# Where eight and eight page loads are issued: behind the compression's last product and at the head of the prompt's stage

## The reference, cut to what matters

```
comp = compress_blocks(...)                       # blocks of 64 rows through a two-layer net with a gelu
o_c, p_c = cmp_attend(q, pos_q, comp, slopes)     # scores on the compressed blocks
idx = select_blocks(sum(p_c), pos_q, nb)          # the 16 best blocks
o_s = slc_attend(q, pos_q, gather_sel(idx), ...)  # attention inside the chosen blocks
o_w = win_attend(q, pos_q, kv_win, pos_win, ...)  # the last 512 tokens
o = gate0 * o_c + gate1 * o_s + gate2 * o_w
```

## Time and profile before

| | |
|---|---|
| median of 3 runs | 907.37 us (906.33 to 907.95) |
| the profiled execution | 907.63 us, of it 905.8 us span |
| TensorE busy | 839.6 us, 93% of the span |
| DVE, ACT, POOL busy | 417.6, 335.0, 129.4 us |
| bytes moved | 102.96 MB, 33.56 MB of them on POOL's queue |
| mean granted TensorE clock | 0.967 of full speed |

### The profile page before, as it was taken

The page is one execution under the profiler, slowest core; times in us unless marked ns, Lnnn a source line. Parts: engine busy times, 40 slices in busy tenths (PEclk is TensorE's granted clock), DMA queues, the critical chain, the costliest instruction groups (busy, mean ns, idle before and its releaser), DMA issues.

```text
span 905.8 us, 17118 instructions
## 1 busy us (share of the span) xinstructions
PE 839.6 (93%) x7279; PEld 760.4 (84%) x7279; DVE 417.6 (46%) x776; ACT 335.0 (37%) x618; POOL 129.4 (14%) x157
## 2 busy tenths in 40 slices
PE   5999998997888878897999999999999999999995
PEld 4999977774555645566999999999999999999995
DVE  5435646665555475565327433344333433243432
ACT  6501155553566564454225431043212331043311
POOL 0001101100784325520220000000000000000120
PEclk9999999997999888998999999999999999999998
DMA  8922638832570206517221122222221122222002
GB/s 299 322 72 94 192 84 272 269 119 93 163 205 8 82 1 233 193 61 189 94 94 41 55 91 93 93 93 93 93 84 37 64 93 93 93 94 93 1 1 105
DMA packets 48789, 102.96 MB, mean 114 GB/s; under 512 B 7498, under 2 KB 19166, under 8 KB 46429
## 3 DMA queue, kind: packets, MB, share of 16 engines
q1 hardware_dynamic: 41821, 68.61, 22.9%
q0 software_dynamic: 6912, 33.56, 11.0%
HBM read 97.75 MB, written 8.53 MB: 117 GB/s over the span
## 4 chain that ended last, share of the span: by engine, by line
PE 52%; DVE 1%; ACT 0%; DVEq 0%; issue 0%
PE banks L1981 51%; PE banks L2022 0%; DVE y L1971 0%; PE banks L2048 0%; DVE wl L1901 0%; PE banks L2038 0%; ACT wh L1845 0%; DVE hT L1939 0%; DVE hT L1914 0%; DVE xl L1918 0%; ACT low L1859 0%; DVE xl L1907 0%; ACT xh L1861 0%; DVEq L1794 0%; ACT small L1889 0%
## 5 line engine op out<-in xcount | busy, mean ns | idle before, releaser
L1981 PE MATMUL banks<-xh,wh 128*128 128x288 f32 x640 | 138.0, 297 | 4.3 <-DVE xl L1907 3.9
L1981 PE MATMUL banks<-xl,wh 128*128 128x288 f32 x640 | 137.8, 297 | 0.0
L1981 PE MATMUL banks<-xh,wl 128*128 128x288 f32 x640 | 137.7, 297 | 0.0
L1845 ACT ACTIVATE wh<-low 128x1024 fp32r<-128x1024 f32 x72 | 75.0, 1050 | 103.1 <-PE banks L1981 102.8
L1981 PE MATMUL banks<-ah,wh 128*128 128x288 f32 x512 | 110.1, 297 | 0.0
L1981 PE MATMUL banks<-ah,wl 128*128 128x288 f32 x512 | 109.7, 296 | 0.0
L1981 PE MATMUL banks<-al,wh 128*128 128x288 f32 x512 | 109.6, 296 | 0.0
L1981 PEld LDWEIGHTS banks<-xh,wh 128*128 128x128 f32 x640 | 103.8, 190 | 4.9 <-DVE wl L1901 4.1
L1981 PEld LDWEIGHTS banks<-xh,wl 128*128 128x128 f32 x640 | 103.9, 190 | 0.0
L1981 PEld LDWEIGHTS banks<-xl,wh 128*128 128x128 f32 x640 | 103.9, 190 | 0.0
L1939 DVE TENSOR_TENSOR hT<-banks,hT 128x288 f32<-128x288 f32 x64 | 26.3, 453 | 138.9 <-PE banks L1981 138.9
(11 more groups left out here) (330 smaller groups left out, 1383.2 us busy)
## 6 DMA issues: line engine op xcount, KB each, us to landing
low<-in_w_up SPq DMA_DIRECT2D x8, 2048.0 KB, 7.8
low<-in_w_down SPq DMA_DIRECT2D x8, 2048.0 KB, 7.7
zone<-in_cmp_w SPq DMA_DIRECT2D x16, 256.0 KB
o_swin<-in_state_win SPq DMA_DIRECT2D x8, 504.0 KB
px<-in_x_prompt SPq DMA_DIRECT2D x4, 512.0 KB, 5.3
u_raw<-in_w_in SPq DMA_DIRECT2D x1, 2048.0 KB, 10.0
q_raw<-in_w_in SPq DMA_DIRECT2D x1, 2048.0 KB, 10.3
low<-in_state_win SPq DMA_DIRECT2D x4, 512.0 KB
```

The source lines that it names most:

```text
L1845: act.activation(wcols(m.wh, i), raw_cols(i), ACT.Copy).then_inc(wh_ready, 1)
L1981: last = pe.matmul(out(i, hf), w[wi], half(x[:, k, :], hf), start=first and part == 0, stop=end and part == 2)
```

## The change

Eight loads of pair 0 go to the end of POOL's part of the compression, behind a new wait on the last product. Eight loads of pair 1 go to the head of POOL's part of the prompt's stage, behind the memset. The loop keeps none. The loads themselves, their places and their semaphores are the same, 16 in all.

```diff
@@ on_gpsimd of compress @@
             load_chunk(pool, m, sems, ck)
+        pool.wait_ge(hid_done, UNITS)
+        for x in range(4):
+            for e in range(2):
+                load_pages(pool, m, 0, e, x, sems)
@@ POOL's part of prompt @@
             pool.memset(m.kc2, 0.0).then_inc(sems.cleared, 1)
-            loads = [(n, e, x) for n in range(2) for x in range(4) for e in range(2)]
+            for x in range(4):
+                for e in range(2):
+                    load_pages(pool, m, 1, e, x, sems)
             for t in range(HPG * U):
                 pool.wait_ge(scl_ready, t + 1)
...
                 last.then_inc(scaled, 1)
-                if 1 <= t <= len(loads):
-                    n, e, x = loads[t - 1]
-                    load_pages(pool, m, n, e, x, sems)
```

## The result

The change takes **922.41 us** (median of 4 runs, 919.39 to 925.77) against 906.85 (905.95 to 907.95) for the kernel before. The ratio is 1.0164, 95% interval 1.0133 to 1.0195: 12 to 18 us slower. The forecast was 911.2, its range 909.2 to 914.6. The kernel of the change was run once more later, beside three of the experiments: 919.87 us (915.57 to 925.40) against 910.23, ratio 1.0117 [1.0074, 1.0159], 7 to 14 us. The sign was right, the size was not.

A forecast was written before the change was run, and what follows sets the result against it. TensorE, busy for 93% of the span, nearly all in the untouched MLP, was taken as the bound. Stage's end 3.5, clock 0.4 and loop -0.1 gave +3.8 us on 907.4, so 911.2; range 909.2 to 914.6.

The forecast's parts named there:

- the loop gives nothing back: Prompt's loop: taking sixteen issues off POOL gains only 0.1 us, bounds 0 and 0.16, as TensorE's rounds are alike.
- Rival 4: Prompt's loop: POOL did set the first round, so freeing it gains 1.7 us, 906.0 in all; chance 0.03.
- the landing waits at the stage's end: Compression's end: the block's drain holds POOL until its own eight loads have landed; taken at +3.5 us.
- rival 1: Compression's end: the stage's end lets the loads fly, only the issue bound of +0.3 us counts, 907.7; chance 0.11.
- the stage's end, +3.5: Compression's end: cost of eight loads behind the last product, from +3.3 to +4.2 by landing time, taken as +3.5 us.
- done 3.9 us after its issue began: Compression's end: landing time from a load that met free DMA engines, putting the eighth load in at 216.1.
- the 0.28 us put behind it: Compression's end: the next stage begins 0.28 us after the last work, as before the change; with the landing, at 216.4.
- middle landing of 6.9 us: Compression's end: landing of loads sharing the DMA engines with others; would make +6.3 us, kept only for the range.
- Rival 2: Compression's end and prompt's head: loads issue slowly, 914.8, or land in 6.9 us, +6.3 and 913.7; chance 0.12.
- the cost is 0, up to 1 us if the issues are slowed: Prompt's head: eight issues take 9.6 to 10.2 us, hidden in POOL's 11.0 us idle.
- rival 3: Gelu: issues hold DVE, 2.1 us; 909.5 without the landing wait, with it an end at 214.9 costing nothing; chance 0.03.
- the clock, +0.4: Prompt's head: added TensorE idle lets part of the first scores run at the lower clock; +0.4 us, bounds -1.0 and +2.0.

The follow-up runs named there:

- the thin: Kernel before plus extra POOL loads of 8 or 16 bytes a row behind the last product, at the prompt's head, or both: ratios 1.0026 to 1.0143.
- the spaced: Kernel before plus eight 8-byte-a-row POOL loads behind the last product, twelve at the prompt's head, three small POOL memsets behind each head load: 920.64 us, ratio 1.0170.
- the memset: Kernel before plus small POOL memsets, 40 behind the last product and 60 behind the prompt's memset, no extra loads: 908.49 us, ratio 1.0005.
- the SP runs: Kernel before plus plain SP transfers of 8 bytes a row, eight behind the last product and twelve at the prompt's head: 906.97 us, ratio 1.0005.
- tail-only run: Kernel of the change with pair 1's eight loads back in the loop, pair 0's still behind the last product: 917.18 us, ratio 1.0091.
- head only: Kernel of the change with pair 0's eight loads back in the loop, pair 1's still at the prompt's head: 912.09 us, ratio 1.0040.
- windows late: Change with pair 0's loads back in the loop and SP's four window loads held until DVE raised scl_ready for the eighth unit: 912.76 us, ratio 1.0036.
- thin 0 + 8: Kernel before plus eight extra POOL loads of 8 bytes a row at the prompt's head, none behind the last product: 910.33 us, ratio 1.0026.
- 8 + 12: Kernel before plus extra POOL loads of 8 bytes a row, eight behind the last product and twelve at the prompt's head: 921.80 us, ratio 1.0143.
- 0 + 12: Kernel before plus twelve extra POOL loads of 8 bytes a row at the prompt's head, none behind the last product: 918.88 us, ratio 1.0126.
- after: The kernel of the change itself, against the kernel before: 922.41 us, ratio 1.0164.
- both without drain: Kernel of the change, both groups of eight loads moved, with the first block opened so that its end doesn't drain POOL: 914.02 us, ratio 1.0072.
- thin 8 + 8: Kernel before plus extra POOL loads of 16 bytes a row, eight behind the last product and eight at the prompt's head: 918.06 us, ratio 1.0079.

## Why the prediction was off, by its own steps

**Right: the loop gives nothing back.** -0.1 was forecast; the stretch from the first scaling on was 0.5 to 0.6 shorter, the later rounds 20.37 and 20.38 us against 20.37. Rival 4 is out.

**Right: the landing waits at the stage's end, and rival 1 is out.** The drain was the deciding question. Without it the stage opens with POOL's loads in flight, with it 4.8 us later.

**Wrong in size: the stage's end, +3.5 against +7.0.** The failed step is "done 3.9 us after its issue began", and the 0.28 us put behind it. Forecast, from the last product: the eighth issue at 8.96, bytes in 3.9 later, release 0.28 later. Measured: the eighth issue at 219.18 - 209.92 = 9.26 (+0.3), packets until 225.02, 5.8 after it (+1.9), release at 226.71, 1.7 after them (+1.4). Two things were overlooked. 3.9 was read off when the bytes stopped moving, and the stage doesn't open 0.28 us after that: with eight loads at the tail and the drain kept, eight profiles have 1.60 to 1.74 us from the last packet of POOL's queue to the memset, for rows of 4 KB, 16 and 8 bytes alike. The Trainium skill ("DMA: Bandwidth & Descriptors", section on the anatomy of one DMA on the SWDGE path) says that most of a DMA's fixed cost of about 2 us is the wait until the last byte is confirmed in the target memory. The 1.7 us here, with the meeting of the engines in them, fit that in size; no run shows what fills them. And eight in a row did build a queue: 283 GB/s from the first issue to the last packet (4.19 MB in 14.8 us), not the 423 at which they were issued. The row that said so was on the sheet. The middle landing of 6.9 us was set aside because those loads share the DMA engines; these eight shared them with each other, and the profile's median for them is 6.2:

```profile
low<-in_cache_slc,idx_slc POOLq DMA_INDIRECT x8, 6.2
```

Rival 2's number for this place, +6.3, was nearly right, for its milder reason.

**Wrong: the head, "hidden", 0 against +4.7.** The failed step is "the cost is 0, up to 1 us if the issues are slowed". It asked only whether POOL would be late for its own next work, and POOL wasn't. It didn't ask who else is slower while POOL issues, except in the gelu (rival 3, whose 214.9 is the end of DVE's copies and not of the gelu), and there it looked at the length of instructions that had begun. That reading was correct: the gelu's instructions take 0.71 and 1.50 us beside the issues, as before. What is held is the start of an instruction, not its run, and no row of the kernel before shows it, since in the stretches read no more than two loads stand back to back. In the first profile 3.0 of the 4.7 us are this, in the second hardly any can be seen; the thin, the spaced, the memset and the SP runs show that it comes with POOL's load issues 0.30 us apart, and not with bytes, with POOL's other work or with SP's transfers.

**Mis-sized: the clock, +0.4 against +1.7 and +4.7.** With TensorE idle from 219.2 to 226.7 the head begins at 0.50 and stays there to about 232.3, so the two pairs of scores and the start of the products ran at the lower level. The tail-only run shows this part by itself: the products end 8.97 us after the memset against 7.34, +1.6, with DVE on time. The upper bound of 2.0 held these two, but not the change's second profile, where the level stayed through all products. Why it came back later there isn't known.

**Sum.** 7.0 + 4.7 - 0.6 = 11.1. 907.4 + 11.1 = 918.5 would have been the forecast, between the two sets of runs of the change (ratios 1.0164 and 1.0117). The rest of the first set's distance is most likely the scatter that moved the last product's end, though no run shows that. Three runs of the kernel before, within 1.6 us of each other, had not let it be seen: later its runs went from 902.8 to 913.9. A small slip of the prediction besides: a burst at 1.43 us an issue lasts 13.5 us and not 13.8, which takes some 0.3 us from rival 2's 914.8.

**What stays open.** By what path the issues hold DVE, and whether it is DVE's start or TensorE's signal to it that comes late: the two held instructions both read PSUM and wait for TensorE, and others of the same kind started on time in between (the first copy of the second layer, at 217.41). In five runs DVE started within, or 0.1 us behind, one of the burst's later issues (head only, windows late, thin 0 + 8, 8 + 12 and 0 + 12), in three others 1.7 to 1.8 us after the last (after, both without drain, thin 8 + 8). In the second profile of the change it is 1.8 us as well, 0.2 behind TensorE; there both limits fall together. Each of these kernels but the change has one profile.

## What to carry to other kernels

An end of a block waits for what POOL has in flight: a load issued behind the last piece of work cost issue, bytes and some 1.7 us from the last packet to the next stage, and the nearest price for it is a landing time of loads that queue with others, not the moment when a lone load's bytes stop. An idle issuing engine doesn't make a burst of loads free: look at who must start an instruction during the burst. One load between two pieces of POOL's own work, as in the kernel before, cost nothing here, and neither did a burst of plain transfers from SP. Count what comes behind an idle TensorE too: here the next stage began at half the clock, and in one profile it stayed there up to the first scaling.

## What the runs showed of the hardware that was not expected

- Eight to twelve indirect loads issued by POOL at 0.30 us distance held the start of single DVE instructions that waited for TensorE, for 0.5 to 6.4 us; with 0.76 us between them, 0.1 us. Four held nothing.
- The end of a block came 2.6 to 2.8 us after the last issue even when the loads carried 8 bytes a row, and 1.60 to 1.74 us after the last packet of eight loads, whatever their size.
- With the same idle time of TensorE ahead (7.5 and 7.3 us), its granted clock stayed at 0.50 for some 5.6 us of the next stage in one profile of the change and for all 16 us up to the first scaling in the other.
- An indirect load holds POOL for 0.94 us whether its rows have 4 KB, 16 or 8 bytes; now and then 1.05 (once 1.17), the first behind a memset 1.07 to 1.09.
- SP issued eight plain transfers in 3.69 us and twelve in 7.52, 0.46 and 0.63 us each.
